# Decay sums of a state space recurrence: four 32-row matmuls in place of four 128-row ones

## The chip, the cores and the metric

One core of a Trainium2 chip. The metric is the time of one execution on the device in microseconds (us), the median over runs. The core has five engines with queues of their own: TensorE (PE; its weight loads are shown as PEld), VectorE (DVE), ScalarE (ACT), GpSimd (POOL) and SyncE (SP), which issues most DMAs.

## The reference, cut to what matters

The program is one block with mixture of experts and a second, hybrid block on 512 tokens of width 1024, all in float32. The change touches the second block's state space branch: two directions, 16 heads of 64, two groups, a state of 128, chunks of 128 tokens.

```python
acs = jnp.cumsum((dt * a_coef).reshape(b, nc, q, G, hg), axis=2)      # q = 128, G * hg = 16 heads
...
seg = acs[:, :, :, None] - acs[:, :, None, :]
lmat = jnp.exp(jnp.where(tri[:, :, None, None], seg, -jnp.inf))       # decay from token j to token i, per head
cb = jnp.einsum('bcign,bcjgn->bcijg', cc, bc)
y_diag = jnp.einsum('bcijgh,bcjghp->bcighp', cb[..., None] * lmat, xdt)
y_off = jnp.einsum('bcign,bcghpn->bcighp', cc, h_in) * jnp.exp(acs)[..., None]
```

For `lmat` every partition j needs the sums `acs` of all 128 tokens i of the chunk, for each head. They are laid along the free axis of all partitions by a matmul.

## The kernel before, in words

Each engine runs a list of instructions written out by hand, function after function (`pe_ssm`, `dve_ssm`, `act_ssm`, `pool_ssm`); semaphores order them. PSUM's eight banks form two rings of four: `to_act` (filled by TensorE, emptied by ScalarE) and `to_dve` (emptied by VectorE). `mm` (L213) is the one call of a matmul, `mm.transpose` (L221) that of a transpose, so all of TensorE's rows carry these two lines.

`dve_acs_rows` (L3065) copies the sums of the four own chunks of both directions, 2 x 64 columns, into `acs_own`; TensorE transposes it, so that each of 128 rows holds the sums of one (direction, chunk, head), in the order 64 d + 16 c + h. VectorE multiplies the transposed tile into four copies, `acs_rows` (128 x 512): copy r keeps the rows whose number is r modulo 4, the others are zero (`row_place`). `row_group` (128 x 32) has a column for each group of four rows, with ones in them. A matmul with one such column, broadcast to 128 columns, as weights and `acs_rows` as the other operand gives in all 128 partitions the sums of four heads beside each other: one bank.

`ssm_units` (L2983) goes through direction 0 (two context chunks, then four own chunks) and direction 1 (the same from the end). An own unit takes:

- `dve_ssm`: two multiplies of L3081 (128 x 1024) make `xw` and `xdt`, then the signal `ssm_x`. L3109 twice (the state's share of the output; in direction 1 each is followed by one more L3081), then for each of two halves of the heads an L3081 on the state and its addition L3121, the mask product `dve_ssm_cb` (L3059), and the additions L3131 of the two halves of the output.
- `pe_ssm`: two matmuls with the state (they wait for `ssm_h`), two for the state's update (they wait for `ssm_x`), then `pe_ssm_decays` of the *next* own unit (two small matmuls B x C, four decay matmuls), then two times eight matmuls of 64 columns that weight `xdt`; each eight wait for `ssm_probs`. Only the first unit's decay matmuls stand ahead of it, and the last unit has none behind it.
- `act_ssm`: for each half g of the heads, eight ReLUs (L3185) out of two banks, one Exp (L3189) over 128 x 1024, signal `ssm_exp`. The buffers `decay` are three; the second half of a unit waits for the first L3131 of the unit before (`ssm_y`).
- `pool_ssm`: for each half one product (L3169, 128 x 1024) of the decays with the masked B x C, in place, then `ssm_probs`.

After the last unit `pe_ssm_out` (L3216) projects z, without a wait on the recurrence.

Of the kernel before, what the change touches and what calls it, by code (L numbers as in the profile page):

```python
# [14 lines left out]
P = 128  # L15
T = 512
TT = T // P
# [264 lines left out]
def build(nc, a, table, where, out):  # L282

    ctx = ExitStack()
    with ctx:
# [3 lines left out]
        def sem(name):  # L289
            return ctx.enter_context(nc.semaphore(name))  # L290
# [34 lines left out]
        def part(at, *shape):  # L325

            n = int(np.prod(shape))
            assert at + n <= SCRATCH, (at, shape)
            v = scratch[:, at:at + n]
            if len(shape) == 2:  # L330
                v = v.rearrange("p (a b) -> p a b", b=shape[1])
            if len(shape) == 3:
                v = v.rearrange("p (a b c) -> p a b c", b=shape[1], c=shape[2])
            return v

        def con(name, width=None):
            at, n = where[name]
            return const[:, at:at + (width or n)]
# [13 lines left out]
        ident = con("ident")  # L352
# [5 lines left out]
        to_act = Banks(psum[0:4], sem("act_banks_full"), sem("act_banks_free"))  # L358
        to_dve = Banks(psum[4:8], sem("dve_banks_full"), sem("dve_banks_free"))
# [16 lines left out]
        dve_done = sem("dve_done")  # L376
# [404 lines left out]
        q, kk, v_tok = part(0, 2, T), part(1024, 2, T), part(2048, TT, 512)  # L781
# [1980 lines left out]
        def s_part(*shape):  # L2762
            v = part(s_at[0], *shape)
            s_at[0] += int(np.prod(shape))
            return v


        d_t, d_ta, acs, e_acs, w_end, e_tot = (s_part(2, NC * NH) for _ in range(6))
        SSM_TMP = 10880
# [3 lines left out]
        conv = [part(SSM_TMP + 3072 + i * T, T) for i in range(2)]  # L2773
        decay = [*(part(SSM_TMP + i * 1024, 8, P) for i in range(2)), sel.rearrange("p a t s -> p (a t) s")]
        cb = [part(SSM_TMP + 2048, 2, P), part(SSM_TMP + 4864, 2, P)]
        row_group, row_place, acs_own = part(SSM_TMP + 5120, 32), part(SSM_TMP + 5152, 4), part(SSM_TMP + 5156, 2, 64)
        acs_rows = con("chunk_keep")
        xdt, xw = part(SSM_TMP + 2304, D), part(SSM_TMP + 3328, D)
        y_part = part(SSM_TMP + 4352, T)
# [203 lines left out]
        def ssm_units():  # L2983
            for d in range(2):
                for c in (range(NC - CT, NC) if d == 0 else range(NC - 1, NC - CT - 1, -1)):
                    yield d, c
                for c in (range(TT) if d == 0 else range(TT - 1, -1, -1)):
                    yield d, c
# [12 lines left out]
        def pe_ssm_decays(pe, mm, unit):  # L3001

            d, c = unit
            chunk = slice(c * P, (c + 1) * P)
            pe.wait_ge(to_dve.free, to_dve.room())
            bank = to_dve.fill()
            for g in range(2):
                ins = mm(bank[:, g * P:(g + 1) * P], b_t[:, g, chunk], c_t[:, g, chunk])
                if g:
                    ins.then_inc(to_dve.full, 1)  # L3010
            for q4 in range(4):
                pe.wait_ge(to_act.free, to_act.room())
                bank = to_act.fill()
                group = 16 * d + 4 * c + q4
                mm(bank[:, :], row_group[:, group:group + 1].broadcast_to([P, P]), acs_rows).then_inc(to_act.full, 1)

        def pe_ssm(pe, mm):
            pe.wait_ge(acs_turned.sem, acs_turned.next(pe))
            pe.wait_ge(to_dve.free, to_dve.room())
            bank = to_dve.fill()  # L3020
            mm.transpose(bank[:, 0:P], acs_own.rearrange("p d n -> p (d n)"), ident).then_inc(to_dve.full, 1)
            pe.wait_ge(acs_turned.sem, acs_turned.next(pe))
            n_own = 0
            for d, c in ssm_units():
                own = c < TT
                if own:
                    if n_own == 0:
                        pe_ssm_decays(pe, mm, OWN_UNITS[0])
                    n_own += 1
                    chunk = slice(c * P, (c + 1) * P)  # L3030
                    pe.wait_ge(ssm_h.sem, ssm_h.next(pe))
                    for g in range(2):
                        pe.wait_ge(to_dve.free, to_dve.room())
                        bank = to_dve.fill()
                        mm(bank[:, :], c_t[:, g, chunk],
                           h_state[d][:, 8 * g:8 * g + 8, :].rearrange("p h x -> p (h x)")).then_inc(to_dve.full, 1)
                pe.wait_ge(ssm_x.sem, ssm_x.next(pe))
                for g in range(2):
                    pe.wait_ge(to_dve.free, to_dve.room())
                    bank = to_dve.fill()  # L3040
                    bt = (b_tok[:, c, :] if own else b_ctx[:, c - TT, :])[:, g * P:(g + 1) * P]
                    mm(bank[:, :], bt, xw[:, g * 512:(g + 1) * 512]).then_inc(to_dve.full, 1)
                if own:
                    if n_own < len(OWN_UNITS):
                        pe_ssm_decays(pe, mm, OWN_UNITS[n_own])
                    for g in range(2):
                        pe.wait_ge(ssm_probs.sem, ssm_probs.next(pe))
                        pe.wait_ge(to_dve.free, to_dve.room())
                        bank = to_dve.fill()
                        for i in range(8):  # L3050
                            ins = mm(bank[:, i * 64:(i + 1) * 64], decay[(2 * n_own - 2 + g) % 3][:, i, :],
                                     xdt[:, (8 * g + i) * 64:(8 * g + i + 1) * 64])
                            if i == 7:
                                ins.then_inc(to_dve.full, 1)
# [8 lines left out]
            dve.sem_inc(ssm_cb.sem, 1)  # L3063

        def dve_acs_rows(dve, step):  # L3065
            dve.tensor_copy(acs_own, acs[:, :, 0:64]).then_inc(dve_done, 1)
            dve.tensor_reduce(row_group, ident.rearrange("p (g r) -> p g r", r=4), AX_X, ALU.add).then_inc(dve_done, 1)
            dve.tensor_reduce(row_place, ident.rearrange("p (g r) -> p r g", r=4), AX_X, ALU.add).then_inc(dve_done, 1)
            dve.wait_ge(dve_done, step.next(3))
            dve.sem_inc(acs_turned.sem, 1)  # L3070
            dve.wait_ge(to_dve.full, to_dve.next_full())
            bank = to_dve.take()
            dve.tensor_tensor(acs_rows.rearrange("p (r i) -> p r i", r=4),
                              bank[:, 0:P].rearrange("p (r i) -> p r i", r=1).broadcast_to([P, 4, P]),
                              row_place.rearrange("p (r i) -> p r i", i=1).broadcast_to([P, 4, P]),
                              ALU.mult).then_inc(to_dve.free, 1)
            dve.wait_ge(to_dve.free, to_dve.own_reads())
            dve.sem_inc(acs_turned.sem, 1)

        def dve_ssm(dve, step):  # L3080
            tt = lambda o, x, y, op: dve.tensor_tensor(o, x, y, op)  # L3081
            dve_acs_rows(dve, step)
            dve.wait_ge(xs_ready.sem, xs_ready.next(dve))
            n_own = 0
# [731 lines left out]
        @block.tensor  # L3816
        def _(pe):
            mm = Matmuls(pe)
            pe_turn_inputs(pe, mm)
            pe.wait_ge(silu_ready.sem, silu_ready.next(pe))  # L3820
            pe_first_mods(pe, mm)
            pe_mix(pe, mm)
            pe_project_out(pe, mm)
            pe_norm(pe, mm, m_sq, T, DT)
            pe_rows(pe, mm, NORM_ROWS)
            pe_norm(pe, mm, n2_sq, T, DT)
            pe_route(pe, mm)
            pe_moe(pe, mm)
            pe_extra(pe, mm)
            pe_norm(pe, mm, m_sq, T, DT)  # L3830
            pe_second_norms(pe, mm)
            pe_dt(pe, mm)
            pe_xbc(pe, mm)
            pe_ssm(pe, mm)
            pe_ssm_out(pe, mm)
            for kind in range(2):
                pe_att_in(pe, mm, kind)
                pe_att(pe, mm, kind)
            pe_merge(pe, mm)
            pe_ffn(pe, mm)  # L3840
            pe_out(pe, mm)
            mm.settle()
# [91 lines left out]
```

## Time and profile before

| | |
|---|---|
| three runs | 3472.62 us (median), 3467.89, 3479.99 |
| profiled execution | span 3471.6 us from the first to the last instruction; no other time is given for it. The median run is 1.0 us longer |
| TensorE | busy 3133.7 us (90%), 13,584 matmul records |
| VectorE, ScalarE, GpSimd | busy 1033.8, 531.3, 163.2 us |
| chain that ended last | TensorE 79%, VectorE 7%, DMA 3%, ScalarE 3% |
| own units of the recurrence | from 2031 to 2147 us after the span's start |

A matmul in float32 leaves two records, each with its own weight load. Busy time of TensorE is the union of its records, whose ends are modelled. The profile's chain follows back, from the last instruction, what each step waited for.

### The profile page before, as it was taken

What the parts mean: (1) busy time and instruction counts of PE and PEld (TensorE: products, weight loads), DVE (VectorE), ACT (ScalarE), POOL (GpSimd) and SP (SyncE); (2) the same over time, 40 slices, a digit from 0 to 9 for tenths busy, and PEclk for the clock granted to TensorE, in tenths of its full rate; (3) what the DMA queues carried; (4) which work ended last, traced back from release to release, by engine and by line L of the source; (5) the groups of instructions that cost most, each with busy time, mean ns of one, the idle gap of its engine ahead of it and who ended that gap; (6) DMA issues with size and microseconds to landing.
All of it is one profiled execution on the core that took longest, in us unless ns stands there. A gap on an engine that the chain in (4) does not pass through costs nothing.

```text
span 3471.6 us, 33580 instructions
## 1 busy us (share of the span) xinstructions
PE 3133.7 (90%) x13584; PEld 1521.1 (44%) x13585; DVE 1033.8 (30%) x1917; ACT 531.3 (15%) x1013; POOL 163.2 (5%) x263
## 2 busy tenths in 40 slices
PE   7787869999999999999958978878789999999998
PEld 3544344444433333333325544366365444344444
DVE  6811122332233232233332367044142101221201
ACT  2212121001000100001012242222142000100000
POOL 3200000000000000000000022000000000000000
PEclk9996867999999999999977999976899999999999
DMA  6157246989999999999950100100101122121210
GB/s 200 55 194 262 63 160 229 342 315 336 327 358 352 360 347 356 357 351 360 355 207 25 49 13 1 57 22 1 49 1 37 61 85 85 61 73 61 96 49 24
DMA packets 298857, 584.52 MB, mean 168 GB/s; under 512 B 15229, under 2 KB 23860, under 8 KB 298676
## 3 DMA queue, kind: packets, MB, share of 16 engines
q1 hardware_dynamic: 293312, 567.18, 45.9%
q0 software_dynamic: 4720, 15.01, 1.5%
q8 instruction: 110, 1.80, 0.2%
q14 instruction: 39, 0.32, 0.0%
q10 hardware_dynamic: 676, 0.21, 0.0%
HBM read 576.08 MB, written 4.19 MB: 167 GB/s over the span
## 4 chain that ended last, share of the span: by engine, by line
PE 79%; DVE 7%; DMA 3%; ACT 3%; issue 2%; PEld 1%; SPq 0%; PEldq 0%; DVEq 0%; ACTq 0%
PE psum_all L213 75%; PE psum_all L221 3%; DVE hidden L2426 2%; DMA panels<-in_w_mod 2%; DVE scratch L3081 1%; DVE scratch L3495 1%; ACT scratch L3557 1%; DMA panels<-in_ada_w 1%; PEld psum_all L213 1%; SPq L190 0%; PEldq L230 0%; ACT hidden L449 0%; ACT scratch L3566 0%; ACT scratch L426 0%; DVE scratch L3389 0%
## 5 line engine op out<-in xcount | busy, mean ns | idle before, releaser
L213 PE MATMUL psum_all<-panels,scratch 128*64 128x512 f32 (+3 forms) x5632 | 985.2, 504 | 10.7 <-issue 9.2
L213 PE MATMUL psum_all<-hidden,panels 128*128 128x512 f32 (+1 forms) x1776 | 783.6, 602 | 17.0 <-ACT hidden L449 10.7
L213 PEld LDWEIGHTS psum_all<-panels,scratch 128*64 128x64 f32 (+2 forms) x5632 | 342.2, 132 | 481.3 <-issue 434.7
L213 PEld LDWEIGHTS psum_all<-hidden,panels 128*128 128x128 f32 (+1 forms) x1776 | 340.2, 192 | 446.6 <-issue 434.5
L213 PE MATMUL psum_all<-scratch 128*128 128x64 f32 (+7 forms) x1384 | 267.2, 392 | 46.6 <-DVEq L3097 22.8
L2426 DVE TENSOR_TENSOR hidden<-hidden,psum_all 128x512 f32<-128x512 f32 x264 | 169.7, 684 | 290.4 <-PE psum_all L213 290.4
L213 PE MATMUL psum_all<-scratch,panels 128*128 128x512 f32 (+1 forms) x672 | 250.5, 531 | 2.0 <-DVE resid L3682 1.0
L213 PEld LDWEIGHTS psum_all<-scratch 128*128 128x128 f32 (+2 forms) x1384 | 196.2, 227 | 106.2 <-issue 47.4
L221 PE MATMUL psum_all<-const,scratch 128*128 128x128 f32 (+5 forms) x946 | 149.3, 296 | 66.0 <-ACTq L3569 20.9
L213 PEld LDWEIGHTS psum_all<-scratch,panels 128*128 128x128 f32 x672 | 127.5, 190 | 127.6 <-issue 119.6
L221 PEld LDWEIGHTS psum_all<-const,scratch 128*128 128x128 f32 (+5 forms) x946 | 108.2, 155 | 164.1 <-issue 86.4
L213 PE MATMUL psum_all<-scratch,const 128*128 128x512 f32 (+5 forms) x308 | 117.7, 527 | 53.3 <-ACT scratch L441 23.6
L213 PE MATMUL psum_all<-panels 128*128 128x512 f32 (+2 forms) x448 | 147.7, 490 | 8.4 <-DVEq L1303 3.9
L213 PE MATMUL psum_all<-tokens_r,y_high 64*128 64x512 f32 (+2 forms) x360 | 96.7, 494 | 28.2 <-DVE hidden L2426 26.6
L2198 ACT ACTIVATE scratch<-psum_all 128x512 f32<-128x512 f32 (+1 forms) x49 | 26.7, 545 | 618.2 <-PE psum_all L221 618.2
L213 PE MATMUL psum_all<-panels,hidden 128*128 128x512 f32 (+2 forms) x384 | 111.4, 455 | 7.7 <-ACT hidden L449 7.7
L2416 DVE SCALAR_TENSOR_TENSOR y_low<-psum_all,scratch,y_high 128x512 fp32r<-128x512 f32 (+1 forms) x49 | 33.6, 686 | 271.9 <-ACT y_high L2387 271.9
L213 PEld LDWEIGHTS psum_all<-panels 128*128 128x128 f32 x448 | 75.5, 197 | 80.7 <-issue 70.3
L213 PEld LDWEIGHTS psum_all<-scratch,const 128*128 128x128 f32 x308 | 58.4, 232 | 104.3 <-issue 62.5
L213 PEld LDWEIGHTS psum_all<-tokens_r,y_high 64*128 64x128 f32 (+2 forms) x360 | 36.6, 184 | 143.2 <-DVE hidden L2426 96.7
L2406 DVE TENSOR_SCALAR scratch<-psum_all 128x512 f32<-128x512 f32 (+1 forms) x49 | 30.7, 626 | 217.8 <-PE psum_all L213 217.8
L2933 DVE TENSOR_SCALAR scratch<-psum_all,cols 128x512 f32<-128x512 f32 (+1 forms) x44 | 33.0, 750 | 197.4 <-PE psum_all L213 197.4
(339 smaller groups left out, 2067.5 us busy)
## 6 DMA issues: line engine op xcount, KB each, us to landing
panels<-in_exp_w_gu SPq DMA_DIRECT2D x132, 2048.0 KB, 11.9
panels<-in_exp_w_down SPq DMA_DIRECT2D x66, 2048.0 KB, 14.2
panels<-in_w_in SPq DMA_DIRECT2D x17, 2048.0 KB, 7.9
panels<-in_w_mod SPq DMA_DIRECT2D x24, 1024.0 KB, 5.2
panels<-in_ada_w SPq DMA_DIRECT2D x16, 1024.0 KB, 6.5
panels<-in_ffn_w_gate SPq DMA_DIRECT2D x5, 2048.0 KB, 9.0
panels<-in_ffn_w_up SPq DMA_DIRECT2D x5, 2048.0 KB, 7.7
panels<-in_ada_w SPq DMA_DIRECT2D x4, 2048.0 KB, 20.8
```

Source lines behind the costliest of these rows:

```text
L213: ins = self.pe.matmul(out, lhsT, rhs, start=start, stop=stop)
L221: return self.pe.transpose(out, in_, ident)
L2198: act.activation(moe_act_t[:, cols], bank[:, 0:cols.stop - cols.start], ACT.Copy).then_inc(moe_t.free, 1)
L2406: dve.tensor_scalar(gb[:, cc], bank[:, 0:cc.stop - cc.start], LIMIT, None, ALU.min)\
L2416: dve.scalar_tensor_tensor(y_lo[:, cc], moe_y(no)[:, 0:cc.stop - cc.start], chunk_vals(u - 1, c)[0], y_hi[:, cc].bitcast(F32), ALU.mult, A ...
L2426: dve.tensor_tensor(hidden[:, m, :], hidden[:, m, :], moe_y(no)[:, :], ALU.add).then_inc(shares_free, 1)
L2933: dve.tensor_scalar(dst[:, 0:n], bank[:, 0:n], w[1], bias, ALU.mult, ALU.add).then_inc(dve_done, 1)
L3081: tt = lambda o, x, y, op: dve.tensor_tensor(o, x, y, op)
L3495: dve.tensor_reduce(tmp_max[:, 0:1], pair[:, 512 - w:768], AX_X, ALU.max).then_inc(dve_done, 1)
L3557: act.activation(p_sb[u % 2][:, 0:w + CTX], att_pairs[u % 2][:, 512 - w:768], ACT.Exp, bias=neg_max[n % 2][:, h:h + 1], scale=HD ** -0.5, ...
```

## The change

The rows of `acs_own` are put in another order, 32 q + 16 d + 4 c + j with head h = 4 q + j, so that the heads 4 q to 4 q + 3 of all units stand in the 32 partitions from 32 q. The decay matmul q then reads these 32 partitions alone, of `row_group` and of `acs_rows`, in place of all 128. The other rows gave only zeros before. Number, shape and place of the outputs stay (four banks of `to_act` per unit), and so do the waits and signals. The copy into `acs_own` becomes two, since its pattern needs one more dimension.

```diff
-        row_group, row_place, acs_own = part(SSM_TMP + 5120, 32), part(SSM_TMP + 5152, 4), part(SSM_TMP + 5156, 2, 64)
+        row_group, row_place, acs_own = part(SSM_TMP + 5120, 32), part(SSM_TMP + 5152, 4), part(SSM_TMP + 5156, P)
...
             for q4 in range(4):
                 pe.wait_ge(to_act.free, to_act.room())
                 bank = to_act.fill()
-                group = 16 * d + 4 * c + q4
-                mm(bank[:, :], row_group[:, group:group + 1].broadcast_to([P, P]), acs_rows).then_inc(to_act.full, 1)
+                strip, group = slice(32 * q4, 32 * q4 + 32), 8 * q4 + 4 * d + c
+                mm(bank[:, :], row_group[strip, group:group + 1].broadcast_to([32, P]), acs_rows[strip, :]).then_inc(to_act.full, 1)
...
-            mm.transpose(bank[:, 0:P], acs_own.rearrange("p d n -> p (d n)"), ident).then_inc(to_dve.full, 1)
+            mm.transpose(bank[:, 0:P], acs_own, ident).then_inc(to_dve.full, 1)
...
-            dve.tensor_copy(acs_own, acs[:, :, 0:64]).then_inc(dve_done, 1)
+            for d in range(2):
+                dve.tensor_copy(acs_own.rearrange("p (q d c j) -> p d c q j", q=4, d=2, c=TT)[:, d],
+                                acs[:, d, 0:64].rearrange("p (c q j) -> p c q j", c=TT, q=4)).then_inc(dve_done, 1)
...
-            dve.wait_ge(dve_done, step.next(3))
+            dve.wait_ge(dve_done, step.next(4))
```

TensorE's order in an own unit (the shape is the output's), which is the same before and now; each of the four decay matmuls, `const,scratch`, waits for a free bank:

```order
L213 MATMUL psum_all<-scratch 128x512 [waits dve_banks_free,ssm_h]
L213 MATMUL psum_all<-scratch 128x512 [waits dve_banks_free]
L213 MATMUL psum_all<-scratch 128x512 [waits dve_banks_free,ssm_x]
L213 MATMUL psum_all<-scratch 128x128 [waits dve_banks_free]
L213 MATMUL psum_all<-scratch 128x128
L213 MATMUL psum_all<-const,scratch 128x512 [waits act_banks_free] x4
L213 MATMUL psum_all<-scratch 128x64 [waits dve_banks_free,ssm_probs]
L213 MATMUL psum_all<-scratch 128x64 x7
```

Nothing moved here; only the rows that the four read are fewer.

VectorE's order ahead of the recurrence, where `acs_own`, `row_group`, `row_place` and `acs_rows` are made:

```order
-L3066 COPY scratch<-scratch 128x128
-L3067 TENSOR_REDUCE scratch<-const 128x32
-L3068 TENSOR_REDUCE scratch<-const 128x4
-L3073 TENSOR_TENSOR const<-psum_all,scratch 128x512
+L3067 COPY scratch<-scratch 128x4x4x4 x2
+L3069 TENSOR_REDUCE scratch<-const 128x32
+L3070 TENSOR_REDUCE scratch<-const 128x4
+L3075 TENSOR_TENSOR const<-psum_all,scratch 128x512
```

One copy became two of half the size; the lines behind are two higher. GpSimd's and ScalarE's orders are the same.

## Rows read from the trace of the kernel before

**Rows 1.** Busy time by engine, one turn: engines' us (records), clock, DMA share, GB/s

```profile
2045.73:2058.57 12.84, 11.15 (x52) 6.97 (x52) 8.86 (x11) 6.46 (x18) 5.50 (x3) 1.00 0.01 1
```

The engines are in the order PE, PEld, DVE, ACT, POOL.

**Rows 2.** Chain that ended last, 2031 to 2200: start us, us, engine, output, line

```profile
2031.16 11.11 PE psum_all L213 x52
...
2045.73 9.39 PE psum_all L213 x48
2055.15 0.70 DVE panels L3131
...
2055.98 1.24 DVE scratch L3081
...
2058.57 9.39 PE psum_all L213 x48
...
2095.64 14.08 PE psum_all L213 x52
...
2138.87 60.50 PE psum_all L213 x164
```

**Rows 3.** Timeline of the burst from 2045.73: start, us, engine, line, operation [idle before]

```profile
2047.99 3.60 PE L213 MATMUL psum_all<-const,scratch 128*128 128x512 f32 x8
...
2049.12 2.17 ACT L3185 ACTIVATE scratch<-psum_all,scratch 128x128 f32<-128x128 f32 x8 [4.35 <-PE psum_all L213]
...
2051.43 1.90 PE L213 MATMUL psum_all<-scratch,slots_of_units 128*128 128x64 f32 x16
2052.57 2.35 POOL L3169 TENSOR_TENSOR scratch<-scratch 128x1024 f32<-128x1024 f32 x1 [4.74 <-ACTq L3191]
...
2057.52 3.16 POOL L3169 TENSOR_TENSOR slots_of_units<-slots_of_units,scratch 128x1024 f32<-128x1024 f32 x1 [2.60 <-ACTq L3191]
```

**Rows 4.** TensorE where tiles are smaller: records begun by 2580.7, timelines at 2580 and 30

```profile
L213 PE MATMUL psum_all<-scratch x4: 589/641/693, 2580.1 to 2580.6; 64*128 64x512 f32 x4
2580.64 0.19 PEld L213 LDWEIGHTS psum_all<-scratch 64*128 64x128 f32 x2 [0.24 <-issue]
2581.07 0.19 PEld L213 LDWEIGHTS psum_all<-scratch 64*128 64x128 f32 x2 [0.24 <-issue]
2581.59 0.87 PE L221 MATMUL psum_all<-const,scratch 128*128 128x128 f32 x6
29.88 1.92 PE L213 MATMUL psum_all<-panels,silus 128*32 128x512 f32 x16
```

The shape before the sizes is that of the weights, rows * columns.

**Rows 5.** Timelines of GpSimd, VectorE and ScalarE from 2033 and from 64

```profile
2033.01 2.17 ACT L3185 ACTIVATE scratch<-psum_all,scratch 128x128 f32<-128x128 f32 x8
2033.08 2.35 POOL L3169 TENSOR_TENSOR scratch<-scratch 128x1024 f32<-128x1024 f32 x1 [345.66 <-ACTq L3191]
...
2033.98 1.99 DVE L3081 TENSOR_TENSOR scratch<-scratch 128x512 f32<-128x512 f32 x1
...
2036.39 2.35 POOL L3169 TENSOR_TENSOR scratch<-scratch 128x1024 f32<-128x1024 f32 x1 [0.96 <-ACTq L3191]
...
64.61 3.28 DVE L1221 TENSOR_TENSOR scratch<-panels,s_columns 128x256 f32<-128x256 f32 x3
65.30 1.11 POOL L904 TENSOR_TENSOR panels<-s_spare,panels 128x512 f32<-128x512 f32 x1
```

**Rows 6.** Timeline ahead of the recurrence

```profile
2010.80 0.23 DVE L3066 COPY scratch<-scratch 128x128 f32<-128x128 f32 x1 [0.80 <-ACTq L2965]
...
2011.14 0.37 DVE L3068 TENSOR_REDUCE scratch<-const 128x4 f32<-128x128 f32 x1
...
2012.68 0.30 PE L221 MATMUL psum_all<-const,scratch 128*128 128x128 f32 x1 [3.47 <-ACT scratch L2978]
```

**Rows 7.** TensorE at the context units of direction 1: timeline, and a window's busy times

```profile
2083.01 1.98 PE L213 MATMUL psum_all<-scratch 128*128 128x512 f32 x4 [2.21 <-DVEq L3097]
2088.59 3.37 PE L213 MATMUL psum_all<-scratch 128*128 128x512 f32 x4 [3.59 <-DVEq L3097]
...
2088.59:2091.41 2.82, 2.82 (x4) 1.18 (x4) 1.33 (x2) 0.00 (x0) 0.00 (x0) 0.50 0.00 0
```

## The prediction

> **What bounds the kernel now.** I read the chain that ended last first, because the change touches 32 matmuls of 13,584 matmul records: what matters is whether they stand on the path. The recurrence has eight own units (two directions, four chunks), and the chain goes through each in the same turn [rows 2]: a burst of matmuls (9.39 us from 2045.73), the addition of its last result on VectorE (L3131), the two multiplies of L3081 that make `xw` and `xdt` for the next unit (1.24 us each), and the next burst at 2058.57. A turn is 12.84 us. In it TensorE is busy 11.15 us, VectorE 8.86, ScalarE 6.46, GpSimd 5.50, at the full clock [rows 1]. After the last burst the chain stays on TensorE for 60.50 us [rows 2], so an earlier or later last burst moves the end by the same amount.
>
> The decay matmuls of the next unit run inside the burst: 2047.99 to 2051.43, 3.43 us for eight records of 0.43 us (each f32 matmul leaves two) [rows 3]. The weighted values follow them and end the burst. So on TensorE the four matmuls are on the path in bursts 1 to 7, and absent from burst 8. The first unit's four come before burst 1, which starts on VectorE's signal; they are over by then and cost nothing while that holds.
>
> **The change, part by part.**
>
> *The matmul itself.* No row of before has four 32-row tiles. The nearest rows are attention's two 64-row tiles, each 128 wide and 512 long as here: two records start at 2580.1 and two at 2580.6, and the weight loads of later pairs come two at a time, 0.43 apart [rows 4]. Two tiles cost what one cost. The other near row is the modulation row: 16 records of 512 elements on four 32-column tiles take 1.92 us, where one after another they would take 16 x 0.43 = 6.9 [rows 4]; so four at once exist too. I take 2 x 0.43 = 0.86 us for the four matmuls. Changing between forms costs something: the 128-row transposes begin at 2581.59, 0.52 after the load at 2581.07, and two records of 256 elements cost 2 x 0.21; that leaves 0.10. The first pair takes 0.53 instead of 0.43, again 0.10. With the same on entering, 0.3. The piece becomes 1.16 us, 2.27 less. Bounds: 3.43 + 0.3 if nothing overlaps, 1.16 if all does; I take the second, since both near rows overlap fully.
>
> *If TensorE alone counted*: seven bursts x 2.27 = 15.9 us. This is the upper end of the gain.
>
> *ScalarE.* It starts on the decays when the first bank is full, 0.69 us after its second record starts (2048.43 is 2047.99 + 0.43; ScalarE starts at 2049.12, 3.39 after the burst's start) [rows 3]. Now that second record starts at 2.26 + 0.10 + 0.53 = 2.89, so ScalarE starts at 3.58: 0.2 later, although all four banks fill together.
>
> *GpSimd against VectorE* decides the turn. A VectorE multiply with both inputs in SBUF doesn't run beside a GpSimd product. The one that started at 2033.98 took 1.99, where L3131, of the same size but with an input in PSUM, takes 0.70 [rows 2]: it ended 0.54 after the product that ran from 2033.08 to 2035.43. The other way, the product of 2057.52 took 3.16 instead of 2.35, since the second L3081 multiply ran until 2058.46: it ended 2.2 after that [rows 3, 5]. In the Trainium skill, "GPSIMD Engine Reference", the table of facts says the same of VectorE instructions with two SBUF inputs.
>
> Today the first product of a unit (2052.57 to 2054.92) fits into the time in which VectorE waits for TensorE. Now work the turn anew, in us from the burst's start. The last result comes 2.27 earlier, at 9.42 - 2.27 = 7.15, and `xw` asks 0.83 later [rows 2], at 7.98. The first product asks 3.45 after ScalarE's start [rows 3], at 7.03, and holds the interface until 9.38. So `xw` ends at 9.38 + 1.08 = 10.46. The second product asks 3.38 after the second half's start on ScalarE [rows 5] and that starts, with two waits between, some 3.44 after the first: at 10.41, 0.05 before `xw` ends and 0.08 before `xdt` asks at 10.49. If it goes first, it ends at 12.66, `xdt` at 13.74, and the next burst starts at 13.85: **1.0 longer than today**. If `xdt` goes first, it ends at 11.72 and the turn is 11.83, 1.0 shorter. Which one? In an earlier stage GpSimd's L904 asked at 65.30, amid three VectorE multiplies of half the size back to back, and ended at 66.41, long before these were through at 67.89 [rows 5]. It got its turn between two of them. The earlier asker wins there. I take "product first".
>
> *Burst by burst.* Burst 1 (11.11 us): its second half needs the product of 2036.39 to 2038.74 [rows 5], 0.2 later now, so only 0.6 is won there, and the next `xw` then runs into the next product, until 44.37, as late as today: 0.0. Bursts 2 and 3: +1.0 each. Burst 4, before the context units: `xw` ends 1.0 earlier, its product delays the state's multiply: -0.4. Burst 5: +1.0. In the second direction VectorE has two more multiplies per unit, its L3131 ends later, so `xdt` asks before the product: burst 6 -1.0; the product then delays the next unit: burst 7 -0.35. Sum: **+1.3**.
>
> *The clock.* TensorE now works 7.15 + 1.7 us of a turn of 13.85 and then waits 5 us, where it waits 1.7 today. After an idle time of 3.59 the four records from 2088.59 took 3.37 us at a granted clock of 0.50 (1.2 GHz); the same four at 2083.01 took 1.98 [rows 7]. That is 1.4 for a short burst. Burst 5 (14.08, after 3.68 idle) against burst 1 (11.11) gives 3.0 [rows 2]. Bursts 3, 4 and 6 follow 5 us of idle time; I take two of these three at 2.2, the middle: **+4.4**. Bounds: 0, and 5 x 3.0 = 15.
>
> *VectorE's copy.* One copy of 0.23 becomes two of half the size. VectorE is done at 2011.51, but TensorE starts at 2012.68, released by ScalarE [rows 6]. Even two at 0.23 are covered by these 1.1 us. Cost 0. Were the cover gone, 0.25.
>
> Sum: +1.3 + 4.4 = +5.7. The profiled execution's span is 3471.6 and the median 3472.6, so I add to the median: **3478.3 us**, a change of 0.16%. A measurement of this kernel can tell about 0.3% (10.4 us) from no change, so this is "no change".
>
> **The rivals.**
>
> 1. *The whole gain.* In the Trainium skill, "TensorEngine Tiling (Array Packing)", PSUM Bottleneck, it is the emptying of PSUM that may bind after tiling. If that were what binds: ScalarE's 6.46 per turn [rows 1] stay below 12.84 - 2.27 = 10.57, nothing binds, and the time is 3472.6 - 15.9 = 3456.7. The rows speak for GpSimd's products instead. Chance 0.10.
> 2. *`xdt` before the product.* Bursts 2, 3, 5 and 6 give -1.0 each, 4 and 7 -0.75 together: -4.8, with one slow burst 3470. The margin is 0.08 us. Chance 0.27.
> 3. *Slower: TensorE's clock.* If the longer waits let the clock fall before five bursts and each pays 3.0: 1.3 + 15 = +16.3, 3488.9. It decides from three to four bursts on. For it: falls after 3.59 and 3.68 us of idle time. Against: at 2088.59 the price was 1.4, not 3.0, and a turn that grows by it gives TensorE less to wait for. Chance 0.12.
> 4. *No overlap.* Each of the four matmuls has its own wait on a free bank, as the order shows, which the near rows don't have. Then they take 3.43 + 0.3: seven times 0.3, 3474.7. Chance 0.08.
>
> The forecast itself has 0.43.
>
> **How the numbers follow.** Only rival 1, and the end of rival 2, lie beyond -10.4: faster 0.13. Rival 3 and the upper tail of the forecast lie beyond +10.4: slower 0.12. Same 0.75. The range 3459 to 3487 takes in rivals 2 and 4 and the forecast with one to four slow bursts; it leaves out most of 1 and the end of 3.
>
> **What would show it.** In the changed profile: four decay records starting together, four more 0.5 us later, and the weighted values 1.2 us after the first; ScalarE's L3185 at 3.6 us into a burst; a first GpSimd product that overlaps the `xw` multiply (which then takes some 2.5 us instead of 1.22), a second one between `xw` and `xdt`; turns of 13.8 us in bursts 2 and 3, idle times of TensorE of 5 us, and a granted clock below 1.0 there. Turns of 10.6 us would prove the interface argument wrong, 11.8 the order of asking; decay records one after another prove the overlap wrong.

## The result, and the profile after

The changed kernel is slower: **3497.59 us** (median of five runs, 3491.41 to 3502.3) against 3476.27 before (five runs, 3467.89 to 3479.99), a ratio of 1.0063 with an interval of 1.0047 to 1.0079. I had forecast 3478.3, range 3459 to 3487. The profiled execution took 3502.3 us, its span is 3500.3, so 2.0 us lie around the span.

Busy times of the turn that answers to [rows 1] (the same columns):

```profile
2053.17:2069.42 16.25, 11.29 (x53) 6.94 (x53) 11.65 (x11) 6.46 (x18) 4.68 (x2) 0.82 0.00 1
```

The turn is 3.4 us longer, TensorE is busy as long although its decays take a third, VectorE is busy 2.8 us more with the same 11 instructions, and the granted clock is 0.82 in place of 1.00. The chain of waits, against [rows 2], with the start and the us first:

```profile
2053.17 9.53 PE psum_all L213 x48
...
2063.56 2.39 DVE scratch L3083
...
2065.98 3.34 DVE scratch L3083
2069.42 9.94 PE psum_all L213 x48
...
2086.07 10.14 PE psum_all L213 x48
...
2105.83 3.65 PE psum_all L213 x4
2112.98 10.43 PE psum_all L213 x52
2130.12 8.68 PE psum_all L213 x48
2145.50 9.45 PE psum_all L213 x48
2161.67 66.50 PE psum_all L213 x164
```

`xw` takes 2.39 us and `xdt` 3.34 where each took 1.24. The bursts 2 to 4, 6 and 7 take 8.7 to 10.1 us where they took 9.39, although 2.2 us are saved in each at full clock (the first experiment below), and the last run takes 66.50 in place of 60.50. The last run begins at half clock, and keeps it for longer than the bursts do; these are two windows at its start, in the columns of [rows 1] (from 2180.00 on the clock is 1.00):

```profile
2161.67:2170.00 8.33, 8.33 (x27) 6.27 (x28) 6.20 (x9) 0.00 (x0) 0.00 (x0) 0.50 0.00 0
2170.00:2180.00 10.00, 10.00 (x28) 5.62 (x28) 7.47 (x7) 0.00 (x0) 0.00 (x0) 0.80 0.01 2
```

The timeline of the same burst as above, against [rows 3]:

```profile
2053.17 4.64 PE L213 MATMUL psum_all<-scratch 128*128 128x512 f32 x8 [4.40 <-DVEq L3099]
2057.74 1.24 PE L213 MATMUL psum_all<-const,scratch 32*128 32x512 f32 x8
2059.06 2.17 ACT L3187 ACTIVATE scratch<-psum_all,scratch 128x128 f32<-128x128 f32 x8 [9.54 <-PE psum_all L213]
2062.51 2.35 POOL L3171 TENSOR_TENSOR scratch<-scratch 128x1024 f32<-128x1024 f32 x1 [10.54 <-ACTq L3193]
2063.56 5.75 DVE L3083 TENSOR_TENSOR scratch<-panels,scratch 128x1024 f32<-128x1024 f32 x2
2065.89 2.34 POOL L3171 TENSOR_TENSOR slots_of_units<-slots_of_units,scratch 128x1024 f32<-128x1024 f32 x1 [1.03 <-ACTq L3193]
```

The eight decay records overlap: 1.24 us for what took 3.60. But ahead of them the first 128-row matmuls need 4.57 us where they needed 2.26: half clock. The first product starts at 2062.51 and `xw` runs into it; the second starts at 2065.89, 0.09 before `xdt` could, and gets ahead of it.

To compare kernels I take one stretch of the trace, **from the first context burst to the end of TensorE's last run**. It is 181.8 us before (2017.62 to 2199.37) and 206.0 after (2022.14 to 2228.18): +24.3. The rest of the program varies from profile to profile: behind the stretch lie 1272.2 us before, 1262.4 to 1280.8 in the kernels below, so whole times blur some microseconds. (The two profiled spans differ by 28.7 us, 4.5 of them ahead of the stretch; the medians differ by 21.3.) Where the 24.3 lie:

| | before | after | more |
|---|---|---|---|
| first context burst to burst 2 | 28.11 | 31.03 | +2.9 |
| bursts 2 and 3, turns | 12.84, 12.85 | 16.25, 16.65 | +7.2 |
| burst 4, with context units | 24.22 | 26.91 | +2.7 |
| burst 5 | 17.53 | 17.14 | -0.4 |
| bursts 6 and 7 | 12.85, 12.85 | 15.38, 16.17 | +5.9 |
| last run | 60.50 | 66.50 | +6.0 |

### The profile page after: what moved, and what is told of

Its sections match the earlier page's. It is cut to its first block, busy times and chain, and to the rows that moved or that the text cites. A ratio compares the mean times of both kernels' runs of the same rounds, so it can differ in the third digit from the quotient of the medians.

```text
span 3500.3 us, 33581 instructions
## 1 busy us (share of the span) xinstructions
PE 3133.7 (90%) x13584; PEld 1518.7 (43%) x13585; DVE 1048.0 (30%) x1918; ACT 531.1 (15%) x1013; POOL 160.3 (5%) x263
## 4 chain that ended last, share of the span: by engine, by line
PE 78%; DVE 8%; ACT 3%; DMA 3%; issue 2%; PEld 1%; SPq 0%; PEldq 0%; DVEq 0%; POOL 0%; ACTq 0%; POOLq 0%
PE psum_all L213 75%; PE psum_all L221 3%; DVE hidden L2426 2%; DMA panels<-in_w_mod 2%; DVE scratch L3083 1%; DVE scratch L3497 1%; DMA panels<-in_ada_w 1%; ACT scratch L3559 1%; PEld psum_all L213 1%; SPq L190 0%; PEldq L230 0%; ACT hidden L449 0%; ACT scratch L3568 0%; ACT scratch L426 0%; DVE scratch L3391 0%
## 5 line engine op out<-in xcount | busy, mean ns | idle before, releaser
L213 PE MATMUL psum_all<-scratch 128*128 128x64 f32 (+7 forms) x1384 | 282.4, 406 | 67.2 <-DVEq L3099 41.8
```

The lines of the kernel that those rows point to most:

```text
L213: ins = self.pe.matmul(out, lhsT, rhs, start=start, stop=stop)
```

## The experiments

Theory A is the prediction's mechanism, with the clock as its amplifier: products of GpSimd land on `xw` and `xdt`, TensorE waits 5 us in place of 1.7, and its clock falls. B: the shorter burst or the small tiles let the clock fall by themselves. C: copies and layout. D: the clock is a bystander. Times are medians; the ratio is to the kernel before, whose own median was 3474.2 to 3476.5 in the groups of runs. The stretch is that of the profiled execution.

| kernel | us | ratio, interval | stretch |
|---|---|---|---|
| before | 3476.27 | | 181.8 |
| changed | 3497.59 | 1.0063 (1.0047 to 1.0079) | 206.0 |
| e3 changed, no products | 3461.61 | 0.9962 (0.9947 to 0.9976) | 166.2 |
| e4 before, no products | 3472.43 | 0.9992 (0.9980 to 1.0005) | 181.7 |
| e5 layout, 128 rows | 3477.84 | 1.0005 (0.9992 to 1.0017) | 182.0 |
| e8 two 64-row tiles | 3500.66 | 1.0068 (1.0052 to 1.0084) | 205.8 |
| e7 six fillers | 3477.14 | 1.0008 (0.9997 to 1.0019) | 188.7 |
| e1 `xw` early | 3476.60 | 1.0001 (0.9991 to 1.0012) | 176.2 |
| e6 before, `xw` early | 3481.62 | 1.0022 (1.0011 to 1.0032) | 183.8 |
| e2 both products gated | 3480.51 | 1.0010 (0.9997 to 1.0023) | 184.7 |
| e9 second gated | 3481.97 | 1.0031 (1.0017 to 1.0046) | 186.7 |
| e10 second gated, two fillers | 3471.76 | 0.9999 (0.9987 to 1.0011) | 179.6 |
| e11 the same, fillers throughout | 3470.33 | 0.9987 (0.9977 to 0.9998) | see there |
| e12 before, fillers | 3470.47 | 0.9989 (0.9978 to 1.0001) | see there |

**Without the products.** In both kernels `pool_ssm` loses one instruction, so the weights lack the factor B x C:

```diff
-                    pool.tensor_tensor(own, own, cb[i % 2][:, g:g + 1, :].broadcast_to([P, 8, P]), ALU.mult)\
-                        .then_inc(pool_done, 1)
-                    pool.wait_ge(pool_done, step.next())
                     pool.sem_inc(ssm_probs.sem, 1)
```

> The changed kernel without GpSimd's 16 products of the decays with the masked B x C (the ones of L3171); GpSimd only passes the signal on, so the weights of the output lack that factor. Theory A (the products hold the SBUF interface against VectorE, TensorE waits 5 us, then its clock falls): `xw` and `xdt` take 1.24 us each, bursts 2, 3, 6 and 7 repeat every 10.6 us (7.15 + 0.83 + 2.5 + 0.1), TensorE's granted clock is 1.0 in them, and the time is about 3456 us, 16 below the kernel before. Theory B (the shorter burst or the 32-row tiles themselves let the clock fall, whatever GpSimd does): `xw` and `xdt` take 1.24 too, but bursts still begin at half clock and take 9.5 us; turns of 12.9 us, a final run of TensorE near 66 us, a time of 3472 to 3480.

> The kernel before without GpSimd's 16 products, the same cut; it is the base for the changed kernel without them. Theory A: turns stay 12.84 us, since before the change no product lay on the path except at the first unit; the time is 3470 to 3473, about 15 us above the changed kernel with the same cut. Theory B: the same time here, but at or below that of the changed kernel with the same cut.

Turns of the changed kernel without products, the columns of [rows 1]:

```profile
2049.51:2060.19 10.68, 8.98 (x52) 5.84 (x52) 8.40 (x11) 6.46 (x18) 0.00 (x0) 1.00 0.01 2
2060.19:2070.88 10.69, 8.98 (x52) 5.84 (x53) 8.39 (x11) 6.46 (x18) 0.00 (x0) 1.00 0.00 1
```

A turn is 10.68 us at the full clock, and `xw` with `xdt` together take 2.48. A burst takes 7.23 us where it took 9.39, so 2.16 are saved. The stretch is 166.2 against 181.7: **15.4 us gained**, where 15.9 were worked out for "TensorE alone". The medians show less of it, 10.8 us, and the time is 3461.6 where 3456 was expected; behind the stretch the profile of the first is 2 us longer. In the kernel before the products cost nothing in sum (181.7 against 181.8), in the changed one 39.8. B falls: with the same tiles and an even shorter burst the clock holds.

**The layout alone**: `strip` goes, and the four matmuls read `row_group[:, group:group + 1].broadcast_to([P, P])` and `acs_rows` whole.

> The changed kernel's row order and its two copies into `acs_own`, but the four decay matmuls read all 128 rows again. Theory A: the decays take 3.4 us again, the first product ends before `xw` asks, turns are 12.84 us, and the time is that of the kernel before within 0.3% (3473, 3465 to 3481). Theory C (the copies, the layout or the stages ahead cost the time, since the changed kernel's recurrence began 4.5 us later): 4.5 us or more above the kernel before, and a recurrence that starts 4.5 us later again.

Turns of 12.86 and 12.84, a stretch of 182.0. C falls. That the changed kernel's recurrence began 4.5 us later is not its doing: in the 12 kernels the first context burst with no filler ahead lies anywhere from 2017.4 to 2022.9, in the kernel before without products at 2022.85.

**Part of the saving.** Rows in the order 0, 2, 1, 3 of the head groups, and tiles of 64 rows (the two copies into `acs_own` become eight for it, which the cut leaves out):

```diff
-                strip, group = slice(32 * q4, 32 * q4 + 32), 8 * q4 + 4 * d + c
-                mm(bank[:, :], row_group[strip, group:group + 1].broadcast_to([32, P]), acs_rows[strip, :]).then_inc(to_act.full, 1)
+                place = (0, 2, 1, 3)[q4]
+                strip, group = slice(64 * (place // 2), 64 * (place // 2) + 64), 8 * place + 4 * d + c
+                mm(bank[:, :], row_group[strip, group:group + 1].broadcast_to([64, P]), acs_rows[strip, :]).then_inc(to_act.full, 1)
```

> The changed kernel with 64-row tiles: the decays go in two pairs, each of two tiles side by side, so that about 1.4 us per burst are saved in place of 2.27. Theory A: ScalarE starts as before, xw asks at 8.8 us and still finds the first product (7.0 to 9.4), the second product still gets ahead of `xdt`, so the turn is the same 13.85 plus the price of the clock: nearly the whole loss of the changed kernel with 60% of its saving; time 3488 to 3497. Rival (the loss goes with what is saved, 60% of it): 3486 or less. If the saving went through: 3463.

One burst of it, first window, then records and ScalarE's start in the timeline:

```profile
2053.25:2069.57 16.32, 12.15 (x53) 7.33 (x53) 10.86 (x11) 6.46 (x18) 4.69 (x2) 0.81 0.00 1
```

```profile
2057.82 2.09 PE L213 MATMUL psum_all<-const,scratch 64*128 64x512 f32 x8
2059.15 2.17 ACT L3189 ACTIVATE scratch<-psum_all,scratch 128x128 f32<-128x128 f32 x8 [9.55 <-PE psum_all L213]
```

Decays of 2.09 us, 0.85 more than with four tiles, ScalarE at 5.90 us as with four (5.89), a turn of 16.32 against 16.25. The whole loss for part of the saving: the time is set by where the products lie, not by TensorE's work. The median is 3.7 us above the upper end expected for it.

**The clock's share.** Ahead of `ssm_h`, in later own bursts, TensorE works instead of waiting, in the bank that it fills next:

```diff
+                    if n_own > 1 and c != (0 if d == 0 else TT - 1):
+                        pe.wait_ge(to_dve.free, to_dve.room())
+                        for i in range(6):
+                            mm(to_dve.banks[to_dve.at_write % len(to_dve.banks)][:, :], c_t[:, 0, chunk],
+                               h_state[1 - d][:, 0:8, :].rearrange("p h x -> p (h x)"))
                     pe.wait_ge(ssm_h.sem, ssm_h.next(pe))
```

> The changed kernel, in which TensorE fills its wait before bursts 2, 3, 4, 6, 7 and 8 with six more matmuls of 512 columns (5.2 us at full clock) into the bank that the burst fills anyway. Theory A (of the 24 us that the changed kernel's recurrence takes longer, 18 are bursts and a last run at half clock, 6 are products that lie on the path): `xw` still takes 2.4 us and `xdt` 3.3, but the bursts proper take 7.15 us, turns are 13.85, the last run 60.5. The stretch from the first context burst to the end of the last run: 206 less 18, 188 us, and a time of 3479, 3476 to 3483. Theory D (something else in the bursts is slow, such as the small tiles or the banks; the clock is a bystander): the stretch stays above 200 us and the time near 3497.

Two windows of 14 us over bursts 2 and 3 (the columns of [rows 1]), then the timeline of VectorE and GpSimd behind burst 2:

```profile
2051.50:2065.50 14.00, 14.00 (x65) 8.02 (x63) 11.19 (x11) 6.46 (x18) 4.92 (x3) 1.00 0.00 0
2065.50:2079.50 14.00, 14.00 (x65) 8.16 (x65) 11.63 (x11) 6.46 (x18) 4.69 (x2) 1.00 0.00 1
```

```profile
2058.62 2.35 POOL L3176 TENSOR_TENSOR scratch<-scratch 128x1024 f32<-128x1024 f32 x1 [6.90 <-ACTq L3198]
...
2059.68 5.75 DVE L3088 TENSOR_TENSOR scratch<-panels,scratch 128x1024 f32<-128x1024 f32 x2
...
2062.00 2.35 POOL L3176 TENSOR_TENSOR slots_of_units<-slots_of_units,scratch 128x1024 f32<-128x1024 f32 x1 [1.02 <-ACTq L3198]
```

The collision is untouched (5.75 us for both multiplies), the clock is 1.00, and of 24.3 us **17.3 are gone**; expected were 18. D falls: with 36 more matmuls the recurrence is faster. TensorE's bursts 3 and 4 begin 13.93 us apart (L3116 at 2065.57 and 2079.50).

Not all of the 17.3 is the fillers' doing. Up to the end of burst 1 the two programs are the same, but in this profile the clock came back sooner in the second context burst: its 16 records take 5.01 us from 2027.46 at a clock of 0.70, where the changed kernel's take 6.45 from 2028.06 at 0.53. ScalarE and GpSimd were earlier by that, `xdt` came ahead of the product (3.03 us for both multiplies from 2046.49), and they ended 28.0 us after the first context burst, not 30.9. The fillers then held the results up by 1.52. So 1.5 of the 17.3 us lie there, and 15.8 behind the first fillers. Of the 6.9 left, VectorE's waits for results behind fillers are 3.1 (1.52 in burst 2, 1.59 in burst 7); some 3.8 remain for the collision. Burst 6 of this run answers another question:

```profile
2132.41 1.23 DVE L3088 TENSOR_TENSOR scratch<-panels,scratch 128x1024 f32<-128x1024 f32 x1
...
2132.58 3.25 POOL L3176 TENSOR_TENSOR scratch<-scratch 128x1024 f32<-128x1024 f32 x1 [1.29 <-ACTq L3198]
```

Here `xdt` starts first and the product waits: the order that the prediction gave for burst 6, at full clock. `xdt` ends 11.7 us after the start of the burst, where 11.7 was forecast. In the changed kernel the burst starts at half clock, ScalarE and GpSimd come later against VectorE, VectorE is through with its own work in time, and the product (2141.97) gets ahead of `xdt` again (3.33 us from 2142.07). The slow clock changes the order of asking too.

**`xw` made early**: `make_xw(n + 1)` stands behind the state's update and `dve_ssm_cb`, ahead of the two L3131, in the changed kernel and in the kernel before; the old multiply at the head of the loop goes.

> The changed kernel, in which VectorE makes `xw` of the next unit before it waits for the last two results of this unit (TensorE has read the old one by then, since its product has been taken). Theory A: `xw` takes 1.24 us, 4.8 us into the burst, and collides with nothing in direction 0; `xdt` asks at 7.9, waits for the first product that ends at 9.4, and ends at 10.46: turns of 10.5 us in bursts 2 and 3, 10.8 in direction 1, TensorE waits no longer than before, and its clock stays at 1.0. Time 3459, 3455 to 3464: faster than both kernels. Theory B: the bursts keep their half clock at the start and take 9.5 us; turns near 12.8, time 3472 to 3480.

> The kernel before, in which VectorE makes the next unit's `xw` before it waits for the last two results. Theory A: `xdt` asks at 10.25 us, after the first product and ahead of the second, and ends at 11.5: turns of 11.6 in place of 12.84 in direction 0 and of 11.6 to 12.4 in direction 1, no fall of the clock. The stretch takes 175 to 178 us, as in the changed kernel with the same edit (176.2), so that the four small matmuls then bring next to nothing. Time 3466 to 3471.

The first turns take 10.76 and 11.20 us, `xdt` 1.60 in the first: as expected. But the clock did not hold: burst 4 began at half clock (8.83 us), behind 2.22 us of idle time, and so did a later one behind 4.73 (2124.92). The stretch is 176.2, 5.6 less than before, where the expected time asked for 9 to 17: VectorE is busy 10.27 us of the 11.20, products hold up a state multiply (2.20 for 0.69), and in direction 1, with more such multiplies, turns stay at 13.1 to 14.7. In the kernel before it failed (183.8, expected 175 to 178), although a turn could take 11.59 as expected (from 2066.80): in burst 1 the early `xw` ran into a product (3.42 us from 2047.07) with both L3131 behind it, TensorE waited 3.69 and went into burst 2 at half clock (11.08); the same again from burst 6 to burst 7. A multiply put ahead of others passes on its own wait.

**Gates on GpSimd.** Ahead of both products, or with `if g:` ahead of the second alone, stands

```diff
+                    pool.wait_ge(ssm_x.sem, ssm_x.next(pool, 1 if i % TT else 1 + CT))
```

> The changed kernel, in which GpSimd starts a unit's two products only when VectorE has made that unit's `xw` and `xdt` (signal ssm_x). Nothing is left out. Theory A: `xw` and `xdt` take 1.24 us each again; in direction 0 the products fall into the next burst, where they hold up the state's two multiplies, and the turn is 10.9 to 11.2 us; in direction 1, with two more VectorE multiplies in the burst, 13.3. TensorE waits no longer than before and its clock stays at 1.0 in direction 0. The stretch from the first context burst to the end of the last run takes 174 to 182 us (181.8 in the kernel before), time 3465 to 3473. Theory B (short bursts let the clock fall whatever GpSimd does): turns of 13 us and more in direction 0, time 3480 or more.

> The changed kernel, in which only the second product of a unit waits until VectorE has made that unit's `xw` and `xdt`; the first stays where it is. Nothing is left out. Theory A: `xw` still takes 2.4 us behind the first product, `xdt` 1.24 in place of 3.33, so a turn is 11.8 us (7.15 + 0.83 + 2.5 + 1.24 + 0.1) where the clock holds, 2.1 less than with the second product first. TensorE waits 3 us, between the 1.7 after which its clock held and the 3.6 after which it fell. If it holds, the stretch from the first context burst to the end of the last run is 176 us and the time 3467; with a fall in each turn, 2.3 us more per turn and some 6 in the last run, 195 us and 3486.

> The same, with two more matmuls of 512 columns (1.7 us at full clock) in TensorE's wait before bursts 2, 3, 4, 6, 7 and 8, as in the kernel with six. Theory A: turns of 11.8 us with the clock at 1.0 all through direction 0, a last run of 60.5 us, a stretch of 176 us and a time of 3467, 3463 to 3472, below both kernels. If the time stays within 3 us of the kernel with the gate alone, the clock had held there already.

Two turns with the second product gated, first without fillers (e9), in the next block with two (e10):

```profile
2046.70:2060.23 13.53, 10.68 (x52) 6.54 (x52) 10.35 (x11) 6.47 (x18) 4.70 (x2) 0.87 0.00 1
2060.23:2073.75 13.52, 10.67 (x52) 6.64 (x52) 10.36 (x11) 6.47 (x18) 4.71 (x2) 0.87 0.00 0
```

```profile
2045.54:2057.38 11.84, 10.70 (x57) 6.60 (x57) 10.36 (x11) 6.47 (x18) 4.70 (x2) 1.00 0.01 1
2057.38:2069.22 11.84, 10.70 (x57) 6.60 (x57) 10.36 (x11) 6.48 (x18) 4.71 (x2) 1.00 0.00 0
```

With the second product last, a turn is 11.84 at full clock (expected 11.8): 1.0 less than before, 2.1 less than product first. Without fillers TensorE is idle for 2.85 us of a turn, and the clock falls in every one. That costs 1.7 us each, and 1.7 in the last run (62.20); expected for a fall were 2.3 and 6, so the stretch is 186.7 and not 195. With fillers the clock holds in direction 0, and the stretch is 179.6, 3.6 more than expected. The 176 expected are 181.8 less 1.0 for each of six turns. Bursts 2 and 3 gave that, burst 4 gave 0.4, and burst 5 gave 1.5 (16.03 to burst 6, its first 5 us at half clock), but bursts 6 and 7 gained nothing (12.85 each), since the second product now falls into the next burst and holds up one of the two multiplies that direction 1 has more (2.23 us for 0.69 at 2109.84 and 2122.69). The last run gave back 1.7: the clock fell once more ahead of it, while TensorE was at work (0.50 from 2130 to 2134). The gate on both gives turns of 11.44 where the clock held (expected 10.9 to 11.2) and 12.36 where not, 13.6 in direction 1 (expected 13.3), and nothing over all (184.7, expected 174 to 182).

**Fillers throughout**, in the kernel with the second gate and in the kernel before: four matmuls ahead of the first context unit, two ahead of each other one, two or three ahead of a direction's first own burst.

> The changed kernel with the second product gated behind `xdt` and two filling matmuls before each later own burst, as in the run before, and fillers in the context units too: four matmuls of 512 columns before the first context unit, two before each other one, two or three before the first own burst of a direction. Nothing is left out. Theory A: each context burst takes 2.0 us in place of 3.8 (four times 1.8 = 7 us), burst 5 some 8 in place of 11.4, turns stay 11.8. The stretch from the first context burst to the end of the last run: 165 to 171 us (179.6 in the run before), time 3457 to 3465. Theory D (the clock is a bystander): stretch near 180, time 3472.

> The kernel before with the same fillers ahead of the context units and of the first own burst of each direction, and none elsewhere (its clock holds there). Theory A: 7 us less in the context bursts and 3 less in burst 5, turns stay 12.84: a stretch of 171 to 173 us against 181.8, time 3462 to 3466; about 6 us (seven turns less one, 1.0 each) behind the changed kernel with gate and fillers. Theory D: stretch 182, time 3474.

The fillers of the first unit lie ahead of the first context burst, so these two are compared from the small transpose ahead of it: 186.7 us in the kernel before, 211.1 changed, 184.5 with gate and two fillers, **178.1** and 183.8 here. The gain of 8.6 us shows as 0.9987 (0.9977 to 0.9998). Its interval just ends below 1, as that of no other complete kernel here does; with twelve kernels compared, that is thin evidence for "faster than before". It is 27 us faster than the changed one. Both gained less than expected. In the second the fall from burst 5 to burst 6 is as worked out (14.57 for 17.53), but the context units of direction 1 gave 1.0 and not 3.6, since VectorE's own chain fills them, and the first four fillers, run at half clock, held up the second context burst by 1.4. With the interval of the second reaching 1.0001, which of the two is better is left open by the medians (3470.33, 3470.47); the stretch says the first, by 5.7, from one profile of each.

## Why the prediction was wrong

- **The overlap (2.27 us per burst)**: right. The decays take 1.14 us at full clock in e3, a burst 2.16 less, and the stretch 15.4 less, against the "TensorE alone" of 15.9. The rival "no overlap" is out.
- **ScalarE's start at 3.58**: right once the clock is taken out: 5.89 less the 2.31 that the first matmuls took longer.
- **GpSimd against VectorE, product first**: right in direction 0. `xw` 2.39, the second product 0.09 us ahead of `xdt`, a turn of 13.93 with the clock held (13.85 forecast). The answer hung on 0.05 to 0.09 us, less than such a sum can tell, so there was luck in it; e9 and e10 show the other branch at 11.84.
- **Burst by burst (+1.3)**: too low. With fillers it is 6.9, and some 3.8 without what the fillers hold up. Burst 1 was put at 0.0, and was so in e7, where the clock came back early. In the changed kernel it cost 2.9: there too the second product got ahead of `xdt` (3.32 us), and with that product gated, at the same late clock, 28.67 us remain of the 31.03 (e9; 28.11 before). In bursts 6 and 7 `xdt` was to come first; at the clock that there was it did not. With the clock held it did in burst 6, but not in burst 7 (5.75 us for both multiplies from 2143.86, a turn of 14.5 where 12.5 was put).
- **The clock (+4.4)**: the step that failed. In e7, with the waits filled, 17.3 us came back, 15.8 of them behind the first fillers. The price per burst was right: bursts 2, 3, 4, 6 and 7 took 2.3, 2.7, 2.9, 1.5 and 2.2 us more than the 7.23 of a full clock, where I took 2.2. The count was wrong: I let two of the three bursts 3, 4 and 6 pay, though my own turn left TensorE idle for 5 us ahead of each and [rows 7] showed a fall after 3.59. All three paid, 7.1 in place of 4.4. Bursts 2 and 7, ahead of which I had put no long wait, paid 4.5 more. And the last run, which I left out, took 6.0 more, at half clock for its first 8.3 us and part of the next 10. Together that is 17.6; even the bound, 15, lay below it.
- **The rivals**: number 3 is what happened, with a chance of 0.12, and its 3488.9 still lies 8.7 below the time measured. By its rows it was no rival but a part of the forecast: it needed nothing more than the forecast's own turn.

## What to carry to other kernels

Before a matmul is made cheaper, look at what its time kept apart: here 2.2 us saved per burst moved VectorE's multiplies onto GpSimd's products, and the loss was the same for a smaller saving. Where a change leaves TensorE waiting longer, price the clock for every burst behind such a wait, the last one included, before taking a share of them. Two small levers work: a gate that makes the helper engine wait, and matmuls that fill the wait, and they have to be tried together. Here they took back the loss, and hardly more: the kernel before, with fillers ahead of its context units, came to the same median.

## What the runs showed of the hardware

- Eight records of 512 columns on four 32-row tiles take 1.14 us at full clock, where 128-row ones take 3.60: 3.2 times faster. The Trainium skill, "TensorE: Matmul & The Clock Gate", Why this matters for your kernels, gives 3.07 for four such tiles; the trace agrees.
- The clock held at TensorE idle times of 1.1 to 1.7 us per turn of 10.7 to 12.9 (e3, e10, before) and fell in every turn of 13.5 at 2.85 (e9). The prediction had rows of falls after 3.59 and 3.68 alone. The length of the last gap does not settle it: a burst began at half clock behind 2.03 us (e9, 2046.70) and behind 2.22 (e1, 2072.34), and another at full clock behind 2.21 (before, 2083.01) and behind 2.51 (e2, 2114.12).
- The same instructions can get the clock back at another time: the second context burst took 6.45 us in the changed kernel and 5.01 in e7, though the code ahead of it is the same.
- A multiply with both inputs in SBUF and a product exclude each other for the whole instruction, in both directions, and the one that asks first goes first: at a lead of 0.09 us in the changed kernel, and of 0.01 in e6 (the product at 2047.06, the multiply, 3.42 us long, at 2047.07).
